# Two transformer blocks on one core: the chunked delta-rule scan regrouped, with another order of its products and copies

## The reference

```python
def step(s, inp):
    r_t, k_t, v_t, kk_t, a_t, w_t = inp
    sa = jnp.einsum("dbhij,dbhj->dbhi", s, kk_t)
    s = (s * w_t[..., None, :] - sa[..., :, None] * (kk_t * a_t)[..., None, :]
         + v_t[..., :, None] * k_t[..., None, :])
    y = jnp.einsum("dbhij,dbhj->dbhi", s, r_t) if readout else None
    return s, y
```

## Time and profile before

| | |
|---|---|
| median of 3 runs | 1383.92 us (1374.85 to 1386.88) |
| the profiled execution's own time | 1383.91 us |
| its span | 1382.1 us |
| PE busy | 1291.2 us (93%), DVE 543.4, ACT 340.2, POOL 136.5 |
| PE on the scan's products (L710) | 5664 records, 183.1 us |
| loop of the scan, to the end of `y_sum` | from 183.2 to 402.6 us |
| mean granted PE clock | 0.969 |

### The profile page before, as it was taken

One profiled execution on the slowest core, in us unless ns is written; L12 is line 12 of the kernel. 1 busy time (PEld: TensorE's weight loads), 2 busy tenths in 40 slices (PEclk: granted clock), 3 DMA queues, 4 the chain that ended last, 5 costly groups with the idle time before them and its releaser, 6 DMA issues.

```text
span 1382.1 us, 25933 instructions
## 1 busy us (share of the span) xinstructions
PE 1291.2 (93%) x11356; PEld 949.9 (69%) x11356; DVE 543.4 (39%) x1188; ACT 340.2 (25%) x868; POOL 136.5 (10%) x207
## 2 busy tenths in 40 slices
PE   6999999999979899999989999998899959999996
PEld 2446888999967788888868887665477744445433
DVE  1255233443352799980031723554253150111113
ACT  3334233332320322111011212435421112101101
POOL 0002344554200000120000000000000010000000
PEclk9999999999999999999999999999799969999998
DMA  9600011212154343434343333221012385999992
GB/s 395 278 0 32 2 63 65 95 64 65 66 205 161 122 169 136 165 125 169 122 149 122 122 122 122 91 93 61 1 63 69 131 347 243 415 428 428 427 428 93
DMA packets 18544, 223.08 MB, mean 161 GB/s; under 512 B 2112, under 2 KB 3264, under 8 KB 3968
## 3 DMA queue, kind: packets, MB, share of 16 engines
q1 hardware_dynamic: 18032, 220.05, 40.8%
q0 software_dynamic: 256, 1.06, 0.2%
q10 hardware_dynamic: 144, 0.31, 0.1%
HBM read 220.37 MB, written 1.05 MB: 160 GB/s over the span
## 4 chain that ended last, share of the span: by engine, by line
PE 90%; DVE 3%; DMA 3%; ACT 2%; issue 1%; SPq 0%; ACTq 0%; DVEq 0%
PE ps L589 37%; PE ps L710 13%; PE ps L1129 7%; PE ps L937 6%; PE ps L996 4%; PE ps L1173 4%; PE ps L1044 2%; PE ps L1140 2%; PE ps L1110 2%; DMA mem<-experts 2%; PE ps L1013 1%; PE ps L567 1%; PE ps L688 1%; PE ps L784 1%; PE ps L1027 1%
## 5 line engine op out<-in xcount | busy, mean ns | idle before, releaser
L589 PE MATMUL ps<-mem 128*128 128x256 f32 (+2 forms) x2096 | 523.2, 407 | 19.6 <-DVE mem L1739 8.3
L589 PEld LDWEIGHTS ps<-mem 128*128 128x128 f32 x2096 | 400.3, 192 | 132.0 <-issue 50.2
L710 PE MATMUL ps<-mem 64*64 64x64 f32 (+1 forms) x5664 | 183.1, 222 | 3.9 <-issue 3.7
L710 PEld LDWEIGHTS ps<-mem 64*64 64x64 f32 x5664 | 176.2, 135 | 14.5 <-issue 14.1
L1768 DVE SCALAR_TENSOR_TENSOR mem<-ps,mem 128x189 f32<-128x189 f32 (+2 forms) x352 | 148.2, 431 | 14.8 <-ACT mem L1384 3.9
L1129 PE MATMUL ps<-mem 128*64 128x512 f32 x512 | 111.6, 592 | 0.7 <-ACT mem L1505 0.5
L1129 PEld LDWEIGHTS ps<-mem 128*64 128x64 f32 x512 | 37.3, 137 | 73.1 <-issue 72.4
L1993 DVE TENSOR_TENSOR mem<-ps,mem 128x512 f32<-128x512 f32 x8 | 5.5, 694 | 188.2 <-PE ps L1129 188.2
L937 PE MATMUL ps<-mem 128*128 128x256 f32 x352 | 77.0, 378 | 0.0
L937 PEld LDWEIGHTS ps<-mem 128*128 128x128 f32 x352 | 66.5, 189 | 9.7
L1236 ACT ACTIVATE mem<-ps 128x256 f32<-128x256 f32 x128 | 49.2, 384 | 82.7 <-PE ps L710 80.0
(11 more groups left out here) (252 smaller groups left out, 1233.4 us busy)
## 6 DMA issues: line engine op xcount, KB each, us to landing
mem<-experts SPq DMA_DIRECT2D x48, 2048.0 KB, 17.5
mem<-weights SPq DMA_DIRECT2D x44, 2048.0 KB, 7.8
mem<-late_ada SPq DMA_DIRECT2D x16, 1024.0 KB, 5.1
mem<-weights SPq DMA_DIRECT2D x3, 1536.0 KB, 6.8
mem<-tokens SPq DMA_DIRECT2D x1, 2048.0 KB, 12.2
mem<-consts SPq DMA_DIRECT2D x1, 1504.0 KB, 23.9
...
```

The source lines that it names most:

```text
L589: last = mm(bank(j % banks)[:, 0:nn], w[:, kc, c * P:(c + 1) * P], rr(kc), start=kc == 0, stop=kc == KD - 1)
L710: last = mm(out[hp, j], lhs[hp, j], rhs[hp, j], start=i == 0, stop=i == len(terms) - 1)
```

## The change

The products are regrouped. `heads` now takes both directions at once. Direction 0 keeps its halves, direction 1 is *crossed*: its low rows write the high columns and its high rows the low ones, into the next PSUM bank. Four matmuls in a row so name four different tiles. A named product is still 16 calls, but its result is taken out by one instruction of 128x512 over two banks. Uncrossed remain `X3` and `turned`.

The algebra is other too. The inverse is no longer formed as a matrix after the near part: three factors (`M4TI`, `M2TI`, `MTI`) are applied one after another to the keys (`X1`, `X2`, `X3`), which does not wait for the state. `spread` turns the solution into a full map for a step (row tiles of 64, weights of 128 columns); only `state` (full rows, column tiles of 64) and `read_out` then touch the carried state, which lies with the values in one tensor `VS`, 128 rows deep. From step 4 on `X0` to `X3` and `spread` are twice as wide (128 columns), because the reads go with the keys.

Keys are formed once ahead of the scan (`key_factors` on ACT, `kd` on POOL, `key_removals` on DVE); a step's staging on POOL falls from 14 instructions to 6. SP gets four SBUF to SBUF transfers of 64 KB a step (`place_values`). The token spectrum goes into the loop, one of four heads' tiles a turn (turns 1 to 4), and its normalisation from turn 1 to turn 5. In the tail `t4` takes one addition instead of six instructions.

```diff
+            def place_values(s):
+
...
+                else:
+                    sp.wait_ge(*turn("state_made", s - 2))
+                    if s - 2 >= READ_FROM:
+                        sp.wait_ge(*each_reading("y_made", s - 2))
+                for d in range(2):
+                    for hp, rows in ((0, LOW), (1, HIGH)):
+                        sp.dma_start(VS[s % 2][VALUES[d], d, hp, :, :], VT[chunk_at(s, d) // C][rows, :, :])\
+                            .then_inc(S("values_placed%d" % (s % 2)), 16)
...
                     .then_inc(S("late_ada_in"), 16)
+                if n == 0:
+                    place_values(0)
+                    place_values(1)
+                elif n % 2 == 0 and n // 2 + 1 < STEPS:
...
+            def heads(b, width, lhs, rhs, crossed=True):
+
+                out = over_banks(b, width)
                 for j in range(NJ):
-                    for i, (lhs, rhs) in enumerate(terms):
-                        for hp in (slice(0, 64), slice(64, 128)):
-                            last = mm(out[hp, j], lhs[hp, j], rhs[hp, j], start=i == 0, stop=i == len(terms) - 1)
+                    for hp in (LOW, HIGH):
+                        mm(out[hp, 0, j], lhs[hp, 0, j], rhs[hp, 0, j], start=True, stop=True)
+                    for hp, to in ((LOW, HIGH), (HIGH, LOW)) if crossed else ((LOW, LOW), (HIGH, HIGH)):
+                        last = mm(out[to, 1, j], lhs[hp, 1, j], rhs[hp, 1, j], start=True, stop=True)
                 return last
...
+            def product(name, b, lhs, rhs, width=C, crossed=True):
+
+                heads(b, width, lhs, rhs, crossed).then_inc(turns_of(name), 1)
...
+            def turned(s):
+                if s >= READ_FROM:
+                    waits(s, "M_kept")
+                    product("X0", prep_bank(s, 0), W8, WR[:, :, :, C:3 * C], 2 * C)
+                waits(s, "MT_kept")
+                product("turned", prep_bank(s, 1), RX[s % 2][:, :, :, FIRST], KX[s % 2][:, :, :, C:3 * C], 2 * C,
+                        crossed=False)
...
+            def squares_of_far(s):
+                waits(s, "M_kept", "MT_kept", "X0_kept")
+                product("M2", prep_bank(s, 0), B1, B2)
+                waits(s, "reads_kept", "gram_kept")
+                product("M2T", prep_bank(s, 1), B2, B1)
+
+            def fourths_of_far(s):
...
+            def first_factor(s):
+                waits(s, "X0_kept", "M4T_kept")
+                if s - 1 >= READ_FROM:
+                    pe.wait_ge(S("y_kept"), 2 * (s - READ_FROM))
...
+            def second_factor(s):
+                waits(s, "X1_kept", "M2T_raised")
+                solve(s, "X2", M2TI, XB)
...
+            def third_factor(s):
+                waits(s, "X2_kept", "MT_raised")
+                solve(s, "X3", MTI, X0, crossed=False)
...
+            def spread_solution(s, d):
+
+                if d == 0:
+                    waits(s, "X3_kept", "reads_kept", "gram_kept")
+                else:
+                    waits(s, "for_state0", "for_values0")
+                width = C if s < READ_FROM else 2 * C
+                for j in range(NJ):
+                    o = [bank(CHAIN + hp)[:, j * width:(j + 1) * width] for hp in range(2)]
+                    for hp, rows in ((0, LOW), (1, HIGH)):
+                        mm(o[hp], KX[s % 2][rows, d, j, C:3 * C], RX[s % 2][rows, d, j, C:C + width],
+                           start=True, stop=False)
+                    for hp, rows in ((0, LOW), (1, HIGH)):
+                        last = mm(o[hp], GR[rows, j, 2 * d:2 * d + 2, :].rearrange("p a c -> p (a c)"),
+                                  XB[rows, d, j, 0:width], start=False, stop=True)
+                last.then_inc(turns_of("spread%d" % d), 1)
...
+            def state(s):
+                waits(s, "for_state0", "for_state1", "for_values0", "for_values1")
...
+                else:
+                    waits(s - 1, "state0", "state1")
...
+                pe.wait_ge(S("values_placed%d" % (s % 2)), 64 * (s // 2 + 1))
+                for r in range(2):
+                    for j in range(NJ):
+                        for d in range(2):
+                            at = (r * NJ + j) * C
+                            last = mm(bank(SIDE)[STATE[d], at:at + C], KF[:, d, r, j, FIRST], VS[s % 2][:, d, r, j, :],
+                                      start=True, stop=True)
+                last.then_inc(turns_of("state_made"), 1)
+
+            def read_out(s):
+                waits(s, "for_state1", "for_values1")
...
-                          (ST[s % 2][d], RO[s % 2][d][:, :, 1, :])).then_inc(S("y_made"), 1)
+                        for hp, rows in ((0, LOW), (1, HIGH)):
+                            at = (d * NJ + j) * C
+                            last = mm(bank(CHAIN)[rows, at:at + C], VS[s % 2][:, d, hp, j, :],
+                                      KF[:, d, hp, j, SECOND], start=True, stop=True)
+                last.then_inc(S("y_made"), 1)
...
-            fourths_of_far(0)
+            turned(0)
+            squares_of_far(0)
             channel_spectrum(2)
             channel_spectrum(3)
-            inverse_of_far(0)
-            token_spectrum(0)
-            token_spectrum(1)
+            fourths_of_far(0)
             for i in range(1, STEPS + 1):
-                late_piece(i - 1, 0)
                 if i < STEPS:
-                    grams(i)
-                held(i - 1)
+                    removals(i)
+                if i >= 2:
+                    turn_piece(i - 2, 1)
+                if i < STEPS:
+                    other_removals(i)
+                first_factor(i - 1)
                 if i < STEPS:
                     squares_of_near(i)
-                if i == 1:
-                    waits(0, 1, "R3_kept")
-                    norm_sums("four", squares_f, NJ, TX, 6)
-                halfway(i - 1)
+                second_factor(i - 1)
+                if i <= NJ:
+                    token_spectrum(i - 1, 0)
+                else:
+                    late_piece(i - 1, 0)
                 if i < STEPS:
                     fourths_of_near(i)
-                else:
-                    turn_piece(i - 1, 0)
-                    late_piece(i - 1, 1)
-                removed(i - 1)
+                third_factor(i - 1)
                 if i < STEPS:
+                    part_of_near(i)
+                    turned_keys(i)
+                if i <= NJ:
+                    late_piece(i - 1, 0)
+                elif i < STEPS:
                     inverse_of_near(i)
-                    turn_piece(i - 1, 0)
-                    state(i - 1)
-                if i >= 5:
-                    if i == 5:
-                        pe.wait_ge(*norm_root("four"))
-                    read_out(i - 1)
+                spread_solution(i - 1, 0)
+                if i <= NJ:
+                    inverse_of_near(i)
+                    token_spectrum(i - 1, 1)
+                elif i == NJ + 1:
+                    waits(i - 2, "state0", "state1")
+                    norm_sums("four", squares_f, NJ, TX, SIDE)
                 if i < STEPS:
                     far_part(i)
-                    late_piece(i - 1, 1)
+                spread_solution(i - 1, 1)
+                turn_piece(i - 1, 0)
+                if i < STEPS:
+                    turned(i)
+                    state(i - 1)
                     squares_of_far(i)
+                if i - 1 >= READ_FROM:
+                    read_out(i - 1)
+                late_piece(i - 1, 1)
+                if i < STEPS:
                     fourths_of_far(i)
-                turn_piece(i - 1, 1)
-                if i < STEPS:
-                    inverse_of_far(i)
+            turn_piece(STEPS - 1, 1)
 
             pe.wait_ge(S("y_kept"), 8)
...
+            def key_factors():
+
+                act.wait_ge(S("ka_rest"), 1)
+                act.wait_ge(S("lora_taken"), 16)
+                for d in (1, 0):
+                    for j in range(NJ):
+                        if d == 0 and j == NJ - 1:
+                            act.wait_ge(S("kk_unit"), NJ)
+                        A(kd[1][:, j, :] if d == 1 else factors[j], iclr[:, d, j, :], ACT.Identity, scale=prm("k_a", j),
+                          bias=ka_rest[:, j:j + 1]).then_inc(S("key_factors"), 1)
...
             def keep_removals(s):
...
+                dve.wait_ge(*turn("removals", s))
+                if s >= 1:
+                    dve.wait_ge(*turn("MT_raised", s - 1))
+                masked(B1, over_banks(prep_bank(s, 1), C), near[:, ::-1]).then_inc(turns_of("A_kept"), 1)
+                dve.wait_ge(*turn("removalsT_copied", s))
+                masked(B2, AO, near).then_inc(turns_of("AT_kept"), 1)
...
+            def keep_grams(s):
+                dve.wait_ge(*turn("reads_kept", s))
+                made = over_banks(prep_bank(s, 1), 2 * C)
+                tt(GR[:, :, 0, :], made[:, 0, :, FIRST], bc(grams[:, 1, :, FIRST], P, NJ, C), ALU.mult)
```

(67 more changed lines are left out.)

678 lines of the change are left out of this document (348 added, 330 removed).

## The result

The changed kernel took 1376.5 us at the median of 20 runs (1360.8 to 1387.2), the kernel before 1387.0 on the same chip: a ratio of 0.990, 95% interval [0.988, 0.992]. Two later measurements of the same pair gave 0.987 [0.983, 0.991] and 0.993 [0.989, 0.996]. The first ratio and its interval leave out four of the 20 runs of the changed kernel, which took over 1.5% more than its fastest. So it is about 1% faster, 13 us where 31 were forecast. The sign was right, the size was not, and the time stands inside the range.

The account below looks back on a forecast made before the run. PE's own time was taken to bound the kernel. Ahead of the loop 171.8, turns 4 x 23.0 + 3 x 25.9, charges 3.7 and 3.4, last turn 20.6, small waits 2.4: 371.6, a gain of 30.9 us, so 1353.0 us, range 1338 to 1382.

Parts of the forecast that it names:

- Four tiles side by side: Scan's crossed products: four matmuls in four tiles take 58.6 ns narrow, 112 wide, so 0.47 or 0.90 us a product.
- Rivals 1 and 2: Tiles that share rows take turns: 1408 us, chance 0.08; records start no faster than now: 1388 us, chance 0.07.
- The rule of the Trainium skill: Matmul starts never closer than about 25 ns: four narrow ones need 100 ns, 28 us more, so about 1380 us.
- Spreads: The two spreads of a turn on PE: 32 groups of 118 ns, 3.78 us together, 1.89 us each.
- The waits that appear: PE, no longer full, waits in the loop for masks and copies: 2.4 us a turn early, 3.5 late.
- Rival 3: Hops bind more: 3.5 us more waiting a turn, 1381 us, or 1367 with half; chance 0.17 for 1366 to 1385.
- Single charges: Turn 5: 3.7 us for norm sums, squares and table load; 3.4 us for the spectrum's normalisation ahead of step 6's masks.
- The last turn: From the hop to `X1` through `y_sum`: 19.9 us, and 0.7 for changes of tile shape, 20.6 us.
- Ahead of the loop: Step 0 stands in the projection's gaps; `removals(1)` comes at 171.8 us, against 183.2 for the loop's start before.
- At nothing: SP's 32 transfers of 64 KB: Value transfers beside the loop cost nothing, DMA being idle three quarters of it; without that cover 1 to 2 us a step.
- The clock: Sign of a wrong forecast: granted clock falling to 1.2 GHz in the new waits; before, full in all but the last turn.

Follow-up runs that it names:

- no_dma: Changed kernel with only the first modulation piece loaded and only the values of steps 0 and 1 placed, both reused: 1356.3 us, 0.976 to the kernel before.
- no_loads: Changed kernel with only the first modulation piece loaded and reused, the 64 KB transfers kept: 1357.0 us, 0.980 to the kernel before.
- moves_odd: Changed kernel with the four 64 KB transfers of a step half a turn later, behind the odd modulation piece: 1368.0 us, 0.985 to the kernel before.
- again2: The changed kernel measured once more, with no edit: 1373.1 us, 0.993 to the kernel before.
- quarters: Changed kernel with modulation pieces in four paced 256 KB transfers, values placed behind the odd piece, first piece used later in turns 5 to 7: 1361.2 us, 0.985 to before.

## Why the prediction was right in kind and wrong in size

- **Four tiles side by side**: right. 32 records of a narrow product start in 0.48 us (0.47 forecast), a wide one in 0.8 to 0.9 (0.90). Rivals 1 and 2 are refuted. The rule of the Trainium skill ("TensorE: Matmul & The Clock Gate", "Wait — 56ns, not 53.3ns?"), which has starts no closer than about 25 ns, does not hold for four tiles in turn: these starts are 15 ns apart on the mean.
- **Spreads** (1.89): 1.73 to 1.78. Right, a little better.
- **The waits that appear**: masks 1.2 us early and 0.9 late (1.5 and 1.1 forecast), `spread1` and `W8` 0.4 to 0.6. These are near, but the wait ahead of `M2T` (0.6 forecast) hardly showed: `M2` and `M2T` took 1.25 us together, 0.3 over two products. In no_dma PE waits 1.2 us from the masks of turn 2 to those of turn 3 (2.4 forecast) and works the other 22.0 (20.6 forecast); two tiles of the token spectrum took 2.1 us (1.78 forecast), `state` 1.08 (0.94), `turned` 1.90 (1.79). That these turns take 23.2 and 23.5 us where 23.0 were forecast is in part luck, two misses that cancel. So it is late (the forecast's own terms there add up to about 3.1 us, not 3.5). Rival 3, with 3.5 us more of waiting a turn, is refuted.
- **Single charges**: turn 6 with the normalisation 29.1 in no_dma (25.9 + 3.4 = 29.3). Right. Turn 5 took 26.6 and not 29.6; its 3.7 us was too much.
- **The last turn**: 353.1 to 373.8 in no_dma, 20.7 (20.6 forecast).
- **Ahead of the loop**: too low by 6.4 us (41.2 from the projection's tile to `removals(1)` in no_dma, 34.8 forecast). POOL's products, taken at 1.1 us, take 1.24 us alone and up to 1.7 beside DVE, and DVE's are dearer beside POOL; 3.7 us of wait ahead of `removals(0)` came of it, then 3.4 us at 1.2 GHz, and as much again at `removals(1)`. The timelines of POOL and of DVE:

```profile
121.07 4.96 POOL L2237 TENSOR_TENSOR mem<-mem 128x512 f32<-128x512 f32 x4 [120.62 <-ACT mem L1428]
125.99 1.27 POOL L2241 TENSOR_TENSOR mem<-mem 128x512 f32<-128x512 f32 x1
...
130.12 1.72 POOL L2242 TENSOR_TENSOR mem<-mem 128x512 f32<-128x512 f32 x1
...
142.09 0.62 POOL L2264 TENSOR_TENSOR mem<-mem 128x256 f32<-128x256 f32 x1
```

```profile
127.91 6.16 DVE L1872 TENSOR_TENSOR mem<-mem 128x512 f32<-128x512 f32 x4
```

  These 6.4 us were met by the loop, which was 4 us shorter than forecast, so that the two misses partly cancel in no_dma: luck again.
- **The step that failed** is "At nothing: SP's 32 transfers of 64 KB ... DMA is idle three quarters of that stretch", and beside it what the sum had no term for: PE's own instructions come over the same DMA engines. I asked whether the data would be in time. I didn't ask what else waits for those engines, and what doubling PE's pace does to it. The price was 12.8 us of pauses, and 6.3 us of clock behind them. The larger part comes with the 1 MB loads, which the kernel before had too and which the sum gave no term; the 64 KB transfers by themselves cost 1.2 us (no_loads), and more only right behind a load (moves_odd).
- **The clock** is the condition that the prediction named ("if the granted clock fell to 1.2 GHz in the new waits"). It did, but not in the waits foreseen: in no_dma, turns with mask waits of 1.2 us keep 1.00. It fell behind the pause of 2 to 4 us and the mask wait just ahead of it (in four of the five turns with a pause in again2), behind the norm's wait, and behind the waits of 3.7 and 2.9 us ahead of the loop. Beside no_dma it cost 6.3 us of PE's time. That the pause brings it down is read from its place and from its going with the pause (no_dma, quarters); no run changed the clock alone. What it does to a product is in the timeline of turn 6, where the four records of a group come 0.11 us after the four before, not 0.06:

```profile
323.42 0.35 PE L774 MATMUL ps<-mem 64*64 64x64 f32 x2
323.47 0.32 PE L776 MATMUL ps<-mem 64*64 64x64 f32 x2
323.53 0.35 PE L774 MATMUL ps<-mem 64*64 64x64 f32 x2
```

The sum of it: forecast 234.6; + 2.3 for what was mis-sized in no_dma; + 12.8 pauses; + 6.3 clock; + 0.3 of other waits: 256.3 us. Before had 265.6. The part behind `y_sum` took 979.6 us before and 979.1 here; over three profiles of the changed kernel it took 975.0 to 984.0, so neither a gain nor a loss there can be told. With all of the data gone the whole kernel is at 0.976, where the forecast's 1353.0 / 1383.9 was 0.978; as misses cancel in it, that is no proof of each term.

What stays open is why PE goes on only 2.3 to 2.9 us after a packet of instructions starts, though the packet takes 0.9 to 1.4 us, and what makes it ask for one.
